# First block of each stage takes its input chunks in step for both outputs; the even mixer projects its values first

## What is computed

```python
def even_mixer(h, w_in, pool_w, pool_scale, sgu_ln_g, sgu_ln_b, sgu_w, sgu_b, w_out):
    z = h @ w_in
    a = z[..., :POOL_WIDTH]
    u = z[..., POOL_WIDTH:POOL_WIDTH + SGU_WIDTH]
    v = z[..., POOL_WIDTH + SGU_WIDTH:]
    y_a = pool_mixer(a, pool_w, pool_scale)
    y_b = sgu_mixer(u, v, sgu_ln_g, sgu_ln_b, sgu_w, sgu_b)
    return jnp.concatenate([y_a, y_b], axis=-1) @ w_out
```

## Time and profile before

| | us |
|---|---|
| median of three runs (lowest, highest) | 3973.56 (3965.65, 3975.5) |
| the profiled execution | 3967.82 |
| its span, first to last instruction | 3966.1 |
| TensorE busy | 3522.7 (89%) |
| VectorE busy | 1894.8 (48%) |
| ScalarE busy | 1443.1 (36%) |
| GpSimd busy | 317.8 (8%) |
| mean granted clock of TensorE | 0.939 of 2.4 GHz |

### The profile page before, as it was taken

One profiled execution on the slowest core, in us unless ns is written; L12 is line 12 of the kernel. 1 busy time (PEld: TensorE's weight loads), 2 busy tenths in 40 slices (PEclk: granted clock), 3 DMA queues, 4 the chain that ended last, 5 costly groups with the idle time before them and its releaser, 6 DMA issues.

```text
span 3966.1 us, 42572 instructions
## 1 busy us (share of the span) xinstructions
PE 3522.7 (89%) x17750; PEld 2923.7 (74%) x17750; DVE 1894.8 (48%) x2663; ACT 1443.1 (36%) x2200; POOL 317.8 (8%) x248
## 2 busy tenths in 40 slices
PE   7788898999999986788889999878999976979997
PEld 5667777878888875677667888666887765857886
DVE  5554555747644344445465544344333455333233
ACT  4443444233323243334424323433232344243222
POOL 0000000211001100000011101031001200230001
PEclk9899899999999998899889999989999867989999
DMA  5001114423321120011263332211222200212221
GB/s 193 32 20 48 42 50 157 163 91 123 108 79 68 55 72 32 6 56 57 75 220 117 122 107 88 94 63 67 92 105 90 77 1 11 85 43 85 95 95 66
DMA packets 74495, 321.96 MB, mean 81 GB/s; under 512 B 8896, under 2 KB 17856, under 8 KB 52288
## 3 DMA queue, kind: packets, MB, share of 16 engines
q1 hardware_dynamic: 74304, 319.25, 23.4%
HBM read 303.49 MB, written 15.73 MB: 80 GB/s over the span
## 4 chain that ended last, share of the span: by engine, by line
PE 66%; DVE 16%; ACT 9%; issue 3%; DMA 3%; POOL 2%; SPq 1%; POOLq 0%; ACTq 0%; DVEq 0%
PE psum L647 20%; PE psum L648 19%; PE psum L649 19%; DVE arena L1481 2%; DVE split_weights L618 2%; DMA arena<-w_ada_dram 2%; DVE arena L1413 2%; PE psum L1124 2%; ACT arena L1257 1%; POOL arena L1904 1%; ACT split_weights L607 1%; DVE split_high L1427 1%; PE psum L1150 1%; DVE arena L842 1%; ACT arena L2595 1%
## 5 line engine op out<-in xcount | busy, mean ns | idle before, releaser
L647 PE MATMUL psum<-split_inputs,split_weights 128*128 128x512 f32 (+1 forms) x3080 | 1158.7, 376 | 85.4 <-DVE split_inputs L849 31.6
L648 PE MATMUL psum<-split_inputs,split_weights 128*128 128x512 f32 (+1 forms) x3080 | 1140.4, 370 | 0.0
L649 PE MATMUL psum<-split_inputs,split_weights 128*128 128x512 f32 (+1 forms) x3080 | 1138.3, 370 | 0.0
L647 PEld LDWEIGHTS psum<-split_inputs,split_weights 128*128 128x128 f32 x3080 | 591.7, 192 | 217.7 <-issue 67.2
L618 DVE TENSOR_TENSOR split_weights<-arena,split_weights 128x2048 fp32r<-128x2048 f32 (+3 forms) x246 | 509.2, 2071 | 448.2 <-ACT split_weights L607 447.9
L649 PEld LDWEIGHTS psum<-split_inputs,split_weights 128*128 128x128 f32 x3080 | 591.0, 192 | 97.3
L648 PEld LDWEIGHTS psum<-split_inputs,split_weights 128*128 128x128 f32 x3080 | 592.4, 192 | 93.5 <-issue 3.4
L607 ACT ACTIVATE split_weights<-arena 128x2048 fp32r<-128x2048 f32 (+3 forms) x246 | 413.6, 1683 | 174.8 <-PE psum L649 174.8
L647 PE MATMUL psum<-split_hidden,split_weights 128*128 128x512 f32 (+1 forms) x880 | 324.3, 369 | 0.1
L648 PE MATMUL psum<-split_hidden,split_weights 128*128 128x512 f32 (+1 forms) x880 | 324.1, 368 | 0.0
L649 PE MATMUL psum<-split_hidden,split_weights 128*128 128x512 f32 (+1 forms) x880 | 323.8, 368 | 0.0
(11 more groups left out here) (304 smaller groups left out, 4747.1 us busy)
## 6 DMA issues: line engine op xcount, KB each, us to landing
arena<-w_up_dram SPq DMA_DIRECT2D x44, 1024.0 KB, 4.9
arena<-ffn_up_dram SPq DMA_DIRECT2D x44, 1024.0 KB, 4.8
arena<-w_ada_dram SPq DMA_DIRECT2D x80, 512.0 KB, 3.8
arena<-w_in_dram SPq DMA_DIRECT2D x32, 1024.0 KB, 5.0
arena<-w_down_dram SPq DMA_DIRECT2D x32, 704.0 KB, 4.1
arena<-ffn_down_dram SPq DMA_DIRECT2D x32, 704.0 KB, 4.1
arena<-od_w_in_dram SPq DMA_DIRECT2D x13, 1024.0 KB, 4.8
arena<-w_ada_dram SPq DMA_DIRECT2D x8, 1024.0 KB, 12.8
```

Of the source, the lines that this page charges most:

```text
L647: pe.e.matmul(dst, a[0], b[0], start=i == 0, stop=False)
L648: pe.e.matmul(dst, a[0], b[1], start=False, stop=False)
L649: ins = pe.e.matmul(dst, a[1], b[0], start=False, stop=i == n - 1)
```

## The change

Three parts.

1. *In step.* `mm3_side` runs over the chunks outermost: for chunk k it waits for the gate once and does the three matmuls of every output of the block, each into its own bank. It is used for the first block of each stage: the latents (outputs 0 and 1, latent stream), the first stack's FFN (its two outputs of the latent stream), the even mixer's first input block (four token tiles), the odd mixer's first (kc and vc), both output projections (outputs 0 and 1) and the second stack's FFN (half 0, m 0). The other outputs stay as they were.
2. *The even mixer's order.* The blocks of `ev_w_in` are v, v, a, a, u, u. The norm of v, and the windows, stand after the second block in VectorE's program, with a weight split ahead of windows 0 and 2. TensorE mixes the values and then multiplies the pooled groups between blocks 4 and 5 (`pe_mixed`). ScalarE evicts the pooled groups ahead of block 5's outputs.
3. *The even mixer's low parts.* VectorE makes all eight; GpSimd's four are gone, and the gates of the even output projection are VectorE's.

No matmul, eviction or DMA is added or removed; four subtractions move from GpSimd to VectorE.

The diff, cut:

```diff
-        return step(0, 1536, 256)
+        return step(1024, 1536, 256) + step(0, 1024, 256)
...
+        def mm3_side(products, gates):
+
+            n = len(gates)
+            for k in range(n):
+                pe.wait_ge(*gates[k])
+                last = []
+                for dst, pairs in products:
+                    a, b = pairs[k]
+                    pe.e.matmul(dst, a[0], b[0], start=k == 0, stop=False)
+                    pe.e.matmul(dst, a[0], b[1], start=False, stop=False)
+                    last.append(pe.e.matmul(dst, a[1], b[0], start=False, stop=k == n - 1))
+            return last
...
+                    side = [(l, name, m, LAT) for m in range(mn)] if blk == 0 else []
+                    dst_of = [banks.take(pe, "latent", *key, place=turn6.next()) for key in side]
+                    if side:
+                        last = mm3_side([(ps, [(w(k, m * P, (m + 1) * P), h_part(k, *LAT)) for k in range(DC)])
+                                         for m, ps in enumerate(dst_of)], h_gates(l, 0, LAT))
+                        for key, ins in zip(side, last):
+                            ins.then_inc(*product("latent", *key))
...
+        def pe_side(keys, w, gates):
+
+            dst_of = [banks.take(pe, *key, place=turn6.next()) for key in keys]
+            last = mm3_side([(ps, [(w(k, j * P, (j + 1) * P), h_part(k, *ALL)) for k in range(DC)])
+                             for j, ps in enumerate(dst_of)], gates)
+            for key, ins in zip(keys, last):
+                ins.then_inc(*product(*key))
+
+        def pe_tokens_side(key, w, width, gates):
+            dst_of = [banks.take(pe, *key, tt, place=turn6.next()) for tt in range(TT)]
+            last = mm3_side([(ps[:, 0:width], [(h_part(k, tt * P, (tt + 1) * P), w(k, 0, width)) for k in range(DC)])
+                             for tt, ps in enumerate(dst_of)], gates)
+            for tt, ins in enumerate(last):
+                ins.then_inc(*product(*key, tt))
...
-                for j in range(2):
-                    pe_project((name, 2 * pair + j), w, j * P, h_part, DC, split_gates(site, ALL))
+                gates = [(h_lo, site, ALL, k) for k in range(DC)] if site == "ev_y" else split_gates(site, ALL)
+                if pair == 0:
+                    pe_side([(name, j) for j in range(2)], w, gates)
+                for j in range(2 if pair else 0):
...
         def pe_even(site):
             for b in range(6):
+                if b == 5:
+                    pe_mixed()
                 w = pe_block("ev_w_in", 0, b)
-                if b < 4:
+                if b < 2:
+                    (pe_tokens if b else pe_tokens_side)(("ev_v", b), w, 256, pre_gates(site))
+                    pe_ends(("ev_w_in", 0, b), "ev_v", b, TT - 1)
+                else:
                     for j in range(2):
-                        pe_project(("ev", 2 * b + j), w, j * P, h_part, DC, pre_gates(site))
-                    pe_ends(("ev_w_in", 0, b), "ev", 2 * b + 1)
-                else:
-                    pe_tokens(("ev_v", b), w, 256, pre_gates(site))
-                    pe_ends(("ev_w_in", 0, b), "ev_v", b, TT - 1)
+                        pe_project(("ev", 2 * b - 4 + j), w, j * P, h_part, DC, pre_gates(site))
+                    pe_ends(("ev_w_in", 0, b), "ev", 2 * b - 3)
+
+        def pe_mixed():
             pe.wait_ge(sgu_in, "pool_w")
-            for g in range(GC):
-                ps = banks.take(pe, "pool", g, place=turn6.next())
-                pe.wait_ge(weighed, "pool", g)
-                pe.e.matmul(ps, pw[:, g, :], pool_diff(g), start=True, stop=True).then_inc(*product("pool", g))
             pe.wait_ge(filled, "causal")
             for g in range(GC):
                 ps = banks.take(pe, "mixed", g, place=turn6.next())
...
+            for g in range(GC):
+                ps = banks.take(pe, "pool", g, place=turn6.next())
+                pe.wait_ge(weighed, "pool", g)
+                pe.e.matmul(ps, pw[:, g, :], pool_diff(g), start=True, stop=True).then_inc(*product("pool", g))
...
+                if b == 5:
+                    for g in range(GC):
+                        act_evict(("pool", g), EY[:, g, :], ACT.Copy, scale=vx("pool_scale", g))
...
         def dve_even(site):
-            for b in range(6):
-                dve_prepare()
+            dve_prepare()
+            dve_prepare()
             for tt in range(TT):
                 v = EV[:, tt, :]
-                dve.wait_ge(copied, "ev_v", 5, tt)
+                dve.wait_ge(copied, "ev_v", 1, tt)
...
-            dve.wait_ge(copied, "ev", 3)
             for g, win in enumerate(POOL_WINDOWS):
+                if g % 2 == 0:
+                    dve_prepare()
+                dve.wait_ge(copied, "ev", g)
...
+            dve_prepare()
             dve.wait_ge(sgu_in, "pool_w")
...
-            for k in range(0, DC, 2):
+            dve_prepare()
+            for k in range(DC):
                 hi, lo = h_part(k, *ALL)
                 dve.wait_ge(h_hi, "ev_y", ALL, k)
...
-            pool_split("ev_y", ALL, lambda k: EY[:, k, :])
...
+                    if what == "kc":
+                        pe_side([("od", "kc"), ("od", "vc")], w, pre_gates(site))
+                if b == 0:
+                    pe_ends(("od_w_in", 0, b), "od", what)
+                elif col is None:
```

More of the change, by code:

```diff
@@ L2082, in pe_glu @@
                     w = pe_block("ffn_up", l, half * HALF_FC + m)
-                    for g in range(2):
+                    if (half, m) == (0, 0):
+                        pe_side([("glu", l, half, m, g) for g in range(2)], w, pre_gates(site))
+                    for g in range(2 if (half, m) != (0, 0) else 0):
                         pe_project(("glu", l, half, m, g), w, g * P, h_part, DC, pre_gates(site))
```

49 lines of the change are left out of this document (29 added, 20 removed).

## The result

The changed kernel takes 3945.28 us (median of 6 runs, 3941.37 to 3947.22) for 3973.34 before (median of 6, 3965.65 to 3975.5). The ratio is 0.9933 (95% interval 0.9923 to 0.9944), 26.6 us less; the medians are 28.1 apart. The forecast was 3936, its range 3922 to 3953. The profiled execution took 3944.44 us with a span of 3942.7, 23.4 less than before's 3966.1.

A forecast was written before the change was run, and what follows sets the result against it. TensorE, 66% of the chain of waits, bounds the kernel, so only its idle or low-clock stretches can give. Gains 15.0 + 2.9 + 14.4 = 32.3 us from 3967.8 give 3935.5, rounded to 3936; range 3922 to 3953.

The forecast's parts named there:

- the starts: First blocks run in step in the latents, FFNs and odd mixer: summed gain 15.0 us, without the even stage.
- the even stage: Two terms: 2.9 us from its first block in step, 14.4 us from the reordered even mixer.
- odd output: Odd mixer's output projection, first block in step: 15.65 us long with 7.8 us low clock, gain 1.05 us.
- latents, layer 1: Second layer's latents: TensorE waits until 1447.42 for ScalarE's square, which stands behind the context modulation; gain 0.
- length = 10.88 + 0.47s: In-step block: 48 matmuls at high clock, 10.88 us, plus 0.47 times s, the window's low-clock time in us.
- I let the clock rise at the same moment as now: Assumption for in-step blocks: each keeps the low-clock time of its present window, 3.4 us in the even stage.
- The even stage's first block: Four token tiles in step: 11.52 us of matmuls plus 1.45 for the low clock; gain 2.9 us.
- The middle of the even mixer: TensorE stands from T + 5.4 to T + 15.1 for VectorE's windows, split and bias add; block 5 starts T + 18.85.
- Middle wait gone: Rival: TensorE's wait in the even mixer is hidden or far shorter, 12.4 us more gained, 3923; chance 0.08.
- The starts gain nothing: Rival: weights or evictions hold the in-step first blocks, their gain goes into the next wait, 3953; chance 0.10.
- VectorE the bound: Rival: VectorE's norm, windows and splits make even blocks 3, 4 and output weights 3 to 4 us late, 3946; chance 0.11.
- The clock stays low: Rival: TensorE stays at 1.2 GHz through the in-step blocks, 5.3 us more in each of seven, 4004; chance 0.04.

## Why the prediction was right, and by how much it was off

**The total.** Forecast 32.3 us; measured by the sites of the profile 32.1 (the starts 16.8, below, and the even stage 15.3), by the mean of two profiles each 29.0, by the ratio 26.6, by the medians 28.1. The direction, the mechanism and the range held; the median lies just above the forecast's own range (3928 to 3944). That the sites come so near to the sum is in part luck: the starts gave 1.8 us more than their 15.0, the even stage 2.0 less than its 17.3.

The first pair of spans is 23.4 apart, 8.7 less than the sites. Of that, 1.0 is given back behind two starts: 0.6 in layer 0's FFN (below) and 0.4 in the odd mixer's input from block 1 on (28.1 us from there to 3133.66 in both profiles of before, 28.5 in both of after; the kernel with the even order alone, whose odd mixer is the old one, has 28.75, so the cause is open). The rest lies in stretches that the change does not touch, and there the same program differs by as much: the attention (5.4 against the change; the two profiles of before are 6.5 apart), the odd mixer from 3133.66 to ahead of its output projection at 3476.21 (1.5; 342.5 and 345.4 before, 344.0 and 343.9 after), and layer 0 between latents and FFN (0.8; 784.6 and 780.1 before, 785.4 and 782.9 after). In the odd stretch the eight other kernels have 345.6 to 347.4, more than either; why, no run shows.

**The starts.** Forecast and measured gain, from the windows of the earlier trace rows and of after, or from start to start:

| | forecast | measured |
|---|---|---|
| FFN, layer 1 | 2.75 | 2.6 |
| second FFN, layer 0 | 2.5 | 2.1 |
| second FFN, layer 1 | 1.8 | 2.1 |
| odd output | 1.05 | 2.5 |
| odd input, to block 1 (15.78 to 13.38) | 1.85 | 2.4 |
| FFN, layer 0 | 0.75 | 0.8, and 0.2 left at the layer's end |
| latents, layer 0 (27.02 to 22.76) | 4.3 | 4.3 |
| latents, layer 1 (18.69 and 18.69) | 0 | 0 |

The rule length = 10.88 + 0.47s held within 0.2 us, but for the odd input (0.4), since little but low clock remains. What failed is the s put into it: "I let the clock rise at the same moment as now". It had 12.7 to 14.6 us for the blocks of 512 columns; they took 12.85 to 13.2. The odd output is the one that this mis-sized. With one output at a time and pauses between the chunks its clock was low for 7.5 to 7.7 us (three profiles), in step for 4.0 to 4.9 (nine profiles): there the start in step also brought the rise of the clock forward, which was worth 1.5 us that the sum does not have.

Two sites show where a gain can end. In layer 1's latents the pair is done 5.4 us ahead of the square, as said. In layer 0's FFN the next weights are ready when forecast (block 1 starts 0.8 us sooner), and 0.65 us of that last until 199 us into the stage. There the first matmul of the down projection finds its weights not yet split in the changed kernel:

```profile
1061.98 0.50 PE L647 MATMUL psum<-split_hidden,split_weights 128*128 128x512 f32 x1 [0.49 <-DVE split_weights L618]
```

With this matmul all twelve profiles are within 199.1 and 200.1 us of the stage's first one, with the starts or without; the second profile of the changed kernel, at 199.1, is the one that kept its gain (562.3 us to the next layer for 563.0 and 563.1 before).

**The even stage's first block.** Forecast 12.97 us long, measured 14.23: with the odd output the term of the sum that was mis-sized most. In lost time (length less the matmuls' 10.88 before and 11.52 after) the forecast gain is 2.9 and the measured one 4.4 - 2.7 = 1.7 us. I took 1.45 us for the low clock, from the 3.4 us low of the window before; TensorE ran low until 6.0 us into the block. That need not come of the change: the second profile of before is low for as long in this block (6.2 us), and takes no longer for it:

```profile
2524.27:2539.55 15.28, 14.77 (x48) 10.22 (x49) 10.99 (x14) 6.16 (x8) 0.00 (x0) 0.80 0.12 40
```

15.28 us at a mean clock of 0.80, where the first profile has 15.27 at 0.89. Here, while chunks are waited for, the low clock costs nothing, since the slower matmuls fill the pauses; in step it is paid in full. So the low time of a window with waits, from one profile, is no safe price for the same window without them: of the seven profiles with the token block in step, three have the clock low for 4.1 to 4.2 us (13.4 long) and four for 5.8 to 6.0 (14.1 to 14.2). And I priced this site as a gain only. It is what makes the new order affordable: without it the block takes 20.0 to 20.5 us, which the prediction does not have.

**The middle of the even mixer.** With T the end of block 4 (2581.34), forecast and measured: mixing until T + 3.6 and T + 3.6; pool matmul 0 done T + 4.5 and T + 4.5 (its half of the 1.88 us, less the overlap); windows 3 and 4 done T + 11.9 and T + 11.9 (2593.26); block 5's split T + 14.2 and T + 14.1; pool matmul 2 T + 15.1 and T + 15.1; block 5 T + 18.85 and T + 17.85, its first matmul then stretched by a microsecond. The links held because each was a pass that the earlier trace rows already time, put in the order in which the engine's program has them. The gap behind block 5 was 2.6 us for 2.2, ended by VectorE's low part; the in-step pair took 12.6 us for 11.7, since the clock fell 0.3 us into it, behind that gap, and stayed low for 3.4 us. The pair is the 0.9 us by which the mixer's 13.5 fall short of the forecast 14.4.

**The rivals.** *Middle wait gone* (0.08): the wait was there; taken away, it gives 11.8 to 13.5 us in the stage for the 12.4 of that bound. *The starts gain nothing*: only at the two sites where the working has it. *VectorE the bound*: its norm and splits were in time for blocks 2 to 4, in which no gap shows. *The clock stays low*: it does not. The blocks of 512 columns that start from idle have mean clocks of 0.82 to 0.87, all of it lost at their beginning; once risen the clock stays high until the block's end, although TensorE changes banks every three matmuls. The section of the Trainium skill that I weighed ("TensorE: Matmul & The Clock Gate", "A second HAM failure mode: psum-queue depth-cycling") tells of small pauses between the groups of matmuls. In step there are none, so these runs do not test its case; they show that the change of bank alone does not bring the clock down.

## What to carry to other kernels

- When the first output of a stage is paced by its input, take the chunks in step for as many outputs as bring the work of a chunk up to the time between chunks (here 1.37 us of matmuls for 1.39). Tiles of half the columns need it more (20.5 us for 14.2 here, where outputs of 512 columns took 15.3 to 15.7 for 12.9 to 13.2), so an order that puts them first is to be priced with the start that it gets.
- Where an engine waits for its input, a low clock is hidden in the waits. Take the waits away and it shows: read the low time from more than one profile before it goes into a sum.
- A new order can make two engines wait for each other in turn. Write out which buffer each pass needs back and who frees it: here two matmuls of under 1 us each, moved ahead of one block, were worth about 12 us.
- Ahead of the sum of the gains, ask at each site what ends next. A wait that two engines end within 0.1 us of each other goes only when both are moved.

## What was not expected of the hardware

- The same program has, in a stretch of 650 us with much idling on TensorE, executions of 652 and of 656 to 658 us, with TensorE's busy time 525 to 530. Differences of 5 us between two single profiles are no evidence unless the stretch itself was edited.
- How far into a block the clock stays low differs between executions of the same program (3.4 and 6.2 us into the even stage's first block before, 4.2 and 6.1 us into layer 0's FFN after) and of nearly the same one (high throughout or low for 3.4 us in the output pair). It moved in-step blocks by 0.8 to 1.6 us, as much as some of the edits.
